# A kernel of two transformer blocks on one core: new orders for the first block's mixers, and a router in column tiles

## The chip, the core and the metric

The kernel is one program for one core of a Trainium2 chip. It is written by hand: each engine (PE for matrix products, DVE for vectors, ACT for activation functions, SP for starting transfers) has a list of instructions of its own and waits for semaphores. The metric is the device time of one execution in microseconds, lower is better. The kernel before took 2264.09 us, the median of three runs (2259.77 to 2264.97).

## The reference

256 tokens of width 1024 in float32 go through two blocks of two layers each. The first block, cut to what matters here:

```
for l in range(2):
    z = rms_norm(x, g_mix[l]) @ w_in[l]              # 2840 columns
    y = concat(chunked_spatial_gating(z_a),          # "ga": 4 heads
               rwkv7_time_mix(z_b),                  # "rw": 4 heads, a recurrence over time
               nsa_attention(z_c))                   # "at": 8 heads, compressed, selected, window
    x = x + y @ w_out[l]
    h = rms_norm(x, g_ffn[l])
    x = x + (swiglu(h) if l == 0 else moe_swiglu(h)) # dense, then 8 experts
    x = x + a gated projection of p[l]               # "ple"
```
```
def moe_swiglu(x, router_w, router_b, w1, w3, w2):
    logits = x @ router_w + router_b
    top_v, top_i = lax.top_k(logits, 2)
    gate = sum of one_hot(top_i) * softmax(top_v)
    return sum over e of gate[:, e] * (silu(x @ w1[e]) * (x @ w3[e])) @ w2[e]
```

The second block (other mixers, a dense network of width 2816 in each layer) is the same in both kernels.

## The kernel before, in words

Tokens lie in two tiles of 128 (`i` = 0, 1). The program is a sequence of stages: mixers of layer 0, dense network, ple, mixers of layer 1 (`pe_mixers1(l)`, `act_mixers1(l)`, `dve_mixers1(l)` for both layers), routing, experts, ple, second block. Nothing plans the order: it is written out by hand in these three functions, one list per engine, and each engine runs its list strictly in order. A step is a small function with the name of its engine in front. Steps of one chain on different engines meet through named signals (`wait_ge`, `then_inc`). So the place of a step in a list says what it runs beside, and a step that waits holds everything behind it on its engine.

The mixers. `win(t, i)` is a product of normalised tokens with 384 of the 2840 input columns (152 for the last `t` = 7); `(0,)` and `(1,)` are its two halves, between which other work can stand. `z(t, i)` is ACT's copy out of PSUM. Beside these products run three chains. *ga*: gelu, a layer norm per head (`ga_norm`, `ga_affine`), one mixing product. *rw*: shift and mix (`rw_shift`, `rw_mix`), low-rank products (`rw_lora`), cumulated decays (`rw_cum`), four turns, products within chunks (`rw_prod`), an inverse by five levels (`rw_lx`, copy, `rw_xlx`, `rw_inverse`, next `rw_level`), then `rw_hv`, `rw_solve`, `rw_inside`, `rw_chunks`, `rw_state` 1 and 2, `rw_read`, `rw_out`, `rw_bonus`, `rw_finish`, which signals `rw.out`. *at*: turns of queries and keys, a compressed attention (`at_compress` to `at_cmp_values`), and six units `u` of the selected and the window attention, each `scores`, `mask`, `max`, `exp`, `gate`, `scale`, `turn_w`, `pt`, `values`. When all is there, `turn_mixed1` and `copy_mixed1` turn the results of ga and rw, `wout1_low(i)` multiplies them with half of `w_out`, and `wout1_high(i)` adds the part of the attention once `at.out` is copied.

The routing (layer 1). `pe_route` makes logits in two tiles of tokens: 16 products with the normalised tokens as stationary operand and 8 router columns as moving one. DVE finds the two best experts of each token (`ro_sel`, signal `route.selected`). PE counts tokens per expert and their places by products with triangular and full matrices of ones (`route.counts`). DVE then sorts the experts by their number of tokens (`route.order`, read by SP, which starts the loads of expert weights), finds places and `mo_pick0`, and writes the largest number (`route.most`). Between its waits PE does the ple products of layer 1, `pe_ple_product(0)` and `(1)`. `pe_mo_gather(0)` collects the tokens of the first expert. Then every worker engine reads `route.most` and branches: the usual path is `gathered`. There, `pe_mo_up(g)` for wave 0 waits for the whole first piece of weights (`moe.up0`, 2 MB). The ring holds five pieces.

## Time and profile before

| | |
|---|---|
| median of 3 runs | 2264.09 us |
| profiled execution | 2261.43 us |
| its span | 2260.1 us |
| PE busy | 2166.3 us, 96% of the span |
| DVE busy | 695.9 us, 31% |
| ACT busy | 427.8 us, 19% |
| chain that ended last | PE 87%, DVE 7%, ACT 3%, DMA 1%, issue 1% |

The span is the time from the first to the last instruction in the records. Layer 0's mixers end at about 227 us, layer 1's lie between 504 and 710, the routing between 715 and 740, the experts between 740 and 1460. A float32 product shows as two records. Source lines say little here, as all instructions pass through one helper (line 89), so rows are told apart by time, engine and operands. The granted clock of PE is given as a share of 2.4 GHz; its two levels are 1.00 and 0.50.

### The profile page before, as it was taken

How to read it: one execution, taken by the hardware profiler on the slowest of the kernel's cores; microseconds unless marked ns; L12 is line 12 of the kernel's file. 1: busy time of each engine (PE TensorE's matmuls, PEld its weight loads, DVE VectorE, ACT ScalarE, POOL GpSimd, SP SyncE). 2: the span in 40 equal slices, each digit the busy share in tenths (PEclk: the TensorE clock that was granted, in tenths of full speed). 3: DMA queues.
4: the chain of work that ended last, by engine and by line, in shares of the span. 5: the costliest groups of instructions: out<-in, count | busy, mean ns of one | idle time of the engine just before them, and what ended most of it. 6: DMA issues, size and time to landing. Idle time of an engine off the chain costs nothing.

```text
span 2260.1 us, 28897 instructions
## 1 busy us (share of the span) xinstructions
PE 2166.3 (96%) x12233; PEld 1260.8 (56%) x12233; DVE 695.9 (31%) x1453; ACT 427.8 (19%) x961; POOL 0.2 (0%) x4
## 2 busy tenths in 40 slices
PE   8988999999979999999999999999999999999998
PEld 5664777765755433333333233365677776657775
DVE  2563365223662100110100001035436633730001
ACT  2464000022462000000000001142310002330001
POOL 0000000000000000000000000000000000000000
PEclk9998999999979999999999999999999999999999
DMA  5221985143301999889999999533199631238300
GB/s 223 86 104 73 423 338 198 34 192 132 107 35 73 423 384 395 345 355 424 403 409 423 377 422 396 209 125 111 56 388 390 225 151 71 88 143 331 142 35 19
DMA packets 55431, 523.38 MB, mean 232 GB/s; under 512 B 6400, under 2 KB 6912, under 8 KB 17152
## 3 DMA queue, kind: packets, MB, share of 16 engines
q1 hardware_dynamic: 46080, 471.13, 51.6%
q10 hardware_dynamic: 9216, 50.34, 5.9%
q8 instruction: 99, 1.62, 0.3%
q14 instruction: 36, 0.29, 0.0%
HBM read 520.39 MB, written 1.05 MB: 231 GB/s over the span
## 4 chain that ended last, share of the span: by engine, by line
PE 87%; DVE 7%; ACT 3%; DMA 1%; issue 1%; SPq 0%; DVEq 0%; ACTq 0%
PE ps L89 87%; DVE ring L89 5%; ACT ring L89 2%; DVE stat L89 1%; DVE transposed L89 1%; DVE natural L89 0%; DMA ring<-in_ple_gate 0%; DMA ring<-in_moe 0%; DVE residual L89 0%; ACT L89 0%; DMA constants<-in_const 0%; DVE gates L89 0%; ACT natural L89 0%; ACT z L89 0%; DVE z L89 0%
## 5 line engine op out<-in xcount | busy, mean ns | idle before, releaser
L89 PE MATMUL ps<-ring 128*32 128x512 f32 (+10 forms) x3812 | 538.8, 515 | 12.7 <-issue 5.5
L89 PE MATMUL ps<-ring,transposed 128*128 128x384 f32 (+4 forms) x1408 | 479.0, 497 | 7.6 <-ACT transposed L89 3.5
L89 PE MATMUL ps<-ring,z 128*32 128x512 f32 (+3 forms) x2048 | 475.8, 584 | 0.3 <-ACT z L89 0.3
L89 PE MATMUL ps<-transposed,ring 128*128 128x256 f32 x2112 | 466.4, 379 | 3.9 <-DVE transposed L89 3.9
L89 PEld LDWEIGHTS ps<-transposed,ring 128*128 128x128 f32 x2112 | 401.1, 190 | 84.4 <-issue 33.1
L89 PEld LDWEIGHTS ps<-ring,transposed 128*128 128x128 f32 x1408 | 264.8, 193 | 197.0 <-issue 67.3
L89 PEld LDWEIGHTS ps<-ring 128*32 128x32 f32 (+4 forms) x3812 | 200.0, 129 | 295.2 <-issue 271.9
L89 DVE TENSOR_TENSOR z<-z,ps 128x256 f32<-128x256 f32 (+2 forms) x138 | 57.5, 417 | 895.6 <-ACT z L89 873.7
L89 PEld LDWEIGHTS ps<-ring,z 128*32 128x32 f32 (+2 forms) x2048 | 174.1, 139 | 247.9 <-issue 241.7
L89 ACT ACTIVATE z<-ps 128x256 f32<-128x256 f32 (+2 forms) x143 | 54.9, 384 | 906.5 <-PE ps L89 906.3
L89 ACT COPY z<-ps 128x256 f32<-128x256 f32 (+6 forms) x154 | 63.4, 412 | 625.4 <-PE ps L89 623.9
L89 DVE SCALAR_TENSOR_TENSOR natural<-z,modulation,natural 128x384 f32<-128x384 f32 x160 | 99.0, 619 | 5.6
L89 ACT ACT_TABLE_LOAD x63 | 80.8, 1283 | 9.7 <-DVE routing L89 5.7
L89 ACT ACTIVATE ring<-ring,stat 128x256 f32<-128x256 f32 (+1 forms) x144 | 65.4, 454 | 29.6 <-DVE stat L89 24.6
L89 DVE TENSOR_TENSOR residual<-residual,ps 128x512 f32<-128x512 f32 x44 | 30.2, 687 | 112.9 <-PE ps L89 112.3
L89 PEld LDWEIGHTS ps<-constants,z 128*128 128x128 f32 (+2 forms) x315 | 32.7, 150 | 54.9 <-issue 51.6
L89 DVE SCALAR_TENSOR_TENSOR ring<-ring 128x256 f32<-128x256 f32 (+2 forms) x126 | 59.4, 471 | 4.5
L89 PE MATMUL ps<-diagonal,residual 128*128 128x128 f32 x320 | 41.7, 287 | 15.7 <-DVE diagonal L89 15.7
L89 PE MATMUL ps<-constants,ring 128*128 128x128 f32 (+3 forms) x292 | 39.9, 312 | 14.2 <-ACT ring L89 13.2
L89 PEld LDWEIGHTS ps<-diagonal,residual 128*128 128x128 f32 x320 | 39.9, 200 | 22.1 <-DVE diagonal L89 19.5
L89 PE MATMUL ps<-constants,z 128*128 128x128 f32 (+2 forms) x315 | 49.0, 284 | 2.1 <-DVE natural L89 2.1
L89 ACT COPY ring<-ps 128x512 f32<-128x512 f32 (+5 forms) x78 | 41.1, 527 | 47.7 <-PE ps L89 44.1
(123 smaller groups left out, 901.6 us busy)
## 6 DMA issues: line engine op xcount, KB each, us to landing
ring<-in_moe SPq DMA_DIRECT2D x88, 2048.0 KB, 13.5
ring<-in_ffn SPq DMA_DIRECT2D x66, 1536.0 KB, 14.0
ring<-in_moe SPq DMA_DIRECT2D x88, 1024.0 KB, 12.6
ring<-in_w_in SPq DMA_DIRECT2D x26, 1536.0 KB, 6.4
z<-in_ada ACTq DMA_DIRECT2D x48, 768.0 KB, 6.2
ring<-in_w_out SPq DMA_DIRECT2D x12, 1536.0 KB, 6.7
natural<-in_ada ACTq DMA_DIRECT2D x16, 768.0 KB, 8.3
ring<-in_ple_gate SPq DMA_DIRECT2D x4, 1536.0 KB, 9.7
```

What stands on the lines that cost most here:

```text
L89: self.ins = None if self.book.counting else op(*args, **kw)
```

## The change

The steps of the three lists of `mixers1` stand in another order. The router's logits are made in four column tiles, kept, and summed over the tiles by a second product; three new operations on DVE (`dve_router`) lay out the router's columns. Counts are made before the places and have a signal of their own, and the ple products are split in four and stand elsewhere. The first piece of expert weights is loaded in two parts of 1 MB; the first wave waits for the first part, and for the second (`moe.up0`) behind its fourth k.

```diff
+    rt = Carve(slot(9))
+    rt_weights, rt_sum, rt_parts = rt(KD, 32), rt(NE), rt(SEQ)
+    def dve_router():
+        dve.wait_ge(*outs1(1))
+        dve(V.memset, rt_weights, 0.0)
+        dve(V.tensor_copy, rt_weights[:, :, 0:NE], column(1, "router").rearrange("p (k e) -> p k e", k=KD))
+        dve(V.tensor_reduce, rt_sum, C("ident").rearrange("p (q e) -> p e q", q=4)[:, 0:NE, :], AXX, ALU.add).then_inc("route.router")
     def pe_route():
-        for i in range(NT):
-            for k in range(KD):
-                mm(ps[:, 4, NE * i:NE * i + NE], xt[:, k, i * P:(i + 1) * P], router[:, k, :], k == 0, k == KD - 1)
+        for k in range(KD):
+            q = k % 4
+            mm(ps[32 * q:32 * q + 32, 4, 0:SEQ], rt_weights[:, k, :], xt[:, k, :], k < 4, k >= 4)
+        pe.then_inc("route.parts")
+        pe.wait_ge("route.parts.kept")
+        for i in range(NT):
+            mm(ps[:, 5, NE * i:NE * i + NE], rt_parts[:, i * P:(i + 1) * P], rt_sum)
         pe.then_inc("route.logits")
-        pe_ple_product(0)
+        pe_ple_product(0, 0)
         pe.wait_ge("route.selected")
-        mm(ps[:, 5, 0:NE], C("tri"), ro_sel[:, 0, :])
-        mm(ps[:, 5, NE:2 * NE], C("tri"), ro_sel[:, 1, :], True, False)
-        mm(ps[:, 5, NE:2 * NE], C("ones"), ro_sel[:, 0, :], False, True)
-        mm(ps[:, 5, 2 * NE:3 * NE], C("ones"), ro_sel[:, 0, :], True, False)
-        mm(ps[:, 5, 2 * NE:3 * NE], C("ones"), ro_sel[:, 1, :], False, True)
+        for i in range(NT):
+            mm(ps[:, 5, 2 * NE:3 * NE], C("ones"), ro_sel[:, i, :], i == 0, i == NT - 1)
         pe.then_inc("route.counts")
-        pe_ple_product(1)
+        mm(ps[:, 4, 0:NE], C("tri"), ro_sel[:, 0, :])
+        mm(ps[:, 4, NE:2 * NE], C("tri"), ro_sel[:, 1, :], True, False)
+        mm(ps[:, 4, NE:2 * NE], C("ones"), ro_sel[:, 0, :], False, True)
+        pe.then_inc("route.places")
+        pe_ple_product(0, 1)
+        pe_ple_product(1, 0)
+        pe_ple_product(1, 1)
         pe_mo_gather(0)
...
     def dve_route():
+        dve.wait_ge("route.parts")
+        dve(V.tensor_copy, rt_parts, ps[:, 4, 0:SEQ]).then_inc("route.parts.kept")
         dve.wait_ge("route.logits")
...
+        dve.wait_ge("route.places")
-        dve(V.tensor_tensor, ro_pv, ps[:, 5, 0:2 * NE].rearrange("p (i e) -> p i e", i=NT), ro_sel, ALU.mult)
+        dve(V.tensor_tensor, ro_pv, ps[:, 4, 0:2 * NE].rearrange("p (i e) -> p i e", i=NT), ro_sel, ALU.mult)
...
-                    sp.wait_ge("ple1.product1")
+                    sp.wait_ge("ple1.product11")
...
+            if (n, part) == (0, "up"):
+                by_half = lambda ap: ap[:, at].rearrange("p (h k n) -> p h k n", h=2, k=2)
+                sp.load(by_half(piece(n))[:, :, 0], by_half(src)[:, :, 0], "first", "moe.first")
+                sp.load(by_half(piece(n))[:, :, 1], by_half(src)[:, :, 1], f"{part}{n % RING_PIECES}", f"moe.{part}{n}")
...
+        if g == 0:
+            pe.wait_ge("moe.first")
...
+                if g == 0:
+                    pe.wait_ge("moe.up0")
```

The PE list of the mixers, from `win(2, 0)` on (the words `pe_`, `rw_`, `at_` are left out; `|` marks a half):

```
before: win20|  shift00 shift10  win20|  win21  win30|  shift01 shift11  win30|  win31  win40  turn_lo
        win41|  lora  win41|  win50  cum  ga_mix  win51|  turn0  win51|  turn1  q0raw q1raw  turn2 turn3
        win60|  prod0 prod1  win60|  win61  first  win70|  lx1  win70|  win71|  xlx1  win71|  turn_k
        lx2  q0rot q1rot  xlx2  pairs0 pairs1  lx3  scores0  xlx3  compress  scores1  cmp_turn_pre
        lx4 xlx4  compressed  lx5 xlx5  turn_w0  hv  cmp_scores  scores2  solve  values0  inside
        turn_w1  cmp_turn  turn_g  scores3  values1  chunks  cmp_values1  turn_w2  cmp_values0  state1
        scores4  values2  state2  read  turn_w3  scores5  values3  turn_mixed1  turn_w4  wout_low0
        values4  turn_w5  wout_low1  values5  wout_high0  wout_high1
after:  win20  win21  win30|  shift00 shift10  win30|  shift01  win31|  shift11  win31|  win40  turn_lo
        win41|  lora  win41|  cum  win50  win51  turn0  win60|  turn1 turn2  ga_mix  turn3  win60|
        prod0 prod1  win61|  q0raw q1raw  first  win61|  win70  win71  lx1  turn_k  xlx1  q0rot q1rot
        lx2  pairs0  xlx2  pairs1  lx3  scores0  xlx3  compress  cmp_turn_pre  scores1
        lx4 xlx4  compressed  lx5 xlx5  turn_w0  hv  solve  scores2  inside  values0  cmp_scores
        turn_w1  turn_g  scores3  chunks  values1  turn_w2  state1 state2  scores4  cmp_turn  read
        cmp_values1  values2  cmp_values0  turn_w3  scores5  values3  turn_mixed1  wout_low0  turn_w4
        wout_low1  values4  turn_w5  wout_high0  values5  wout_high1
```

The parts of the other two lists that differ and that the prediction speaks of:

```diff
 ACT
-  z30 z31  ga_gelu  z40  lo_copy  ga_root  wa  z41  rw_root  z50  decays  turn0  z51  turn1 ...
+  z30 z31  lo  z40  lo_copy  wa  ga_gelu  z41  ga_root  rw_root  decays  z50  turn0 ... turn3  z51
-  exp1  cmp_exp  scale1  pt1  exp2  turn_g  cmp_turn  scale2 ...
+  exp1  scale1  cmp_exp  pt1  exp2  turn_g  scale2  pt2  exp3  cmp_turn ...
-  scale3  pt3  norm_root  exp4  scale4  copy_mixed1  pt4
+  scale3  norm_root  pt3  copy_mixed1  exp4  scale4  pt4
 DVE
-  ga_norm ga_affine  wa keys wx keys2 factors  ga_out  rotate_q pairs  prod0 prod1 first level1
+  wa keys  ga_norm  wx keys2 factors  ga_affine ga_out  prod0 prod1 first level1  rotate_q pairs
-  level4  max0  mask1  hidden  inverse4 level5 kp  gate0 max1  inverse5  hv  cmp_mask  mask2  solve
+  level4  max0  hidden  inverse4 level5 kp  mask1  gate0 max1  inverse5  hv  solve  mask2
-  gate1 max2  cmp_weights  inside  mask3 gate2 max3  chunks  state1  mask4  state2  gate3  max4
+  gate1 max2  inside  cmp_mask cmp_weights  mask3 gate2 max3  chunks  state1 state2  mask4  gate3
-  out bonus finish  mask5 ...
+  out bonus finish  max4  mask5 ...
+  if l == 1: dve_router()     # behind gate5
```

## Rows read from the trace of the kernel before

**Rows 1.** Busy time by stage: us from the start: length, each engine, clock, DMA.
```profile
22.00:205.00 183.00, 163.35 (x1466) 111.76 (x1465) 92.88 (x194) 88.46 (x197) 0.00 (x0) 0.93 0.23 85
509.00:693.00 184.00, 163.45 (x1468) 111.57 (x1467) 92.54 (x192) 85.56 (x189) 0.00 (x0) 0.93 0.23 84
741.00:1460.00 719.00, 719.00 (x4763) 254.19 (x4761) 64.67 (x145) 58.69 (x156) 0.00 (x0) 1.00 0.94 387
```

**Rows 2.** PE timeline, layer 1 mixers: start, length, operation, records, [idle before <- releaser].
```profile
611.34 3.05 PE L89 MATMUL ps<-ring 128*32 128x128 f32 x80
...
627.76 6.42 PE L89 MATMUL ps<-ring 64*64 64x64 f32 x72
...
671.04 1.97 PE L89 MATMUL ps<-constants,natural 128*128 128x128 f32 x8 [4.87 <-DVE natural L89]
...
676.96 9.04 PE L89 MATMUL ps<-ring,transposed 128*128 128x512 f32 x16
```

**Rows 3.** DVE timeline of the same stretch, columns as above.
```profile
616.62 1.42 DVE L89 TENSOR_TENSOR ring<-ps,constants 128x512 f32<-128x512 f32 x2
...
628.96 0.69 DVE L89 COPY z<-ps 128x512 f32<-128x512 f32 x1 [1.96 <-PE ps L89]
632.85 0.41 DVE L89 TENSOR_TENSOR ring<-ps,constants 128x240 f32<-128x240 f32 x1 [3.19 <-PE ps L89]
...
649.35 0.94 DVE L89 COPY ring<-ps 128x128 f32<-128x128 f32 x3
...
659.03 1.26 DVE L89 TENSOR_TENSOR ring<-ring,ps 64x128 f32<-64x128 f32 x4
...
673.02 1.22 DVE L89 TENSOR_REDUCE stat<-ring 128x4 f32<-128x1024 f32 x1
```

**Rows 4.** ACT timeline of the same stretch, columns as above.
```profile
643.19 1.20 ACT L89 COPY ring<-ps 128x512 f32<-128x512 f32 x2 [1.19 <-PE ps L89]
...
673.02 2.13 ACT L89 ACTIVATE ring<-ring,stat 128x256 f32<-128x256 f32 x4 [5.31 <-DVE stat L89]
675.23 1.26 ACT L89 COPY transposed<-ps 128x512 f32<-128x512 f32 x2
...
695.97 0.58 ACT L89 COPY transposed<-ps 128x512 f32<-128x512 f32 x1 [6.69 <-PE ps L89]
```

**Rows 5.** Busy time of two windows, columns as in rows 1.
```profile
634.12:642.06 7.94, 7.12 (x133) 6.00 (x133) 6.33 (x15) 3.62 (x9) 0.00 (x0) 0.84 0.01 2
720.00:727.00 7.00, 7.00 (x18) 3.35 (x17) 2.01 (x9) 0.96 (x3) 0.00 (x0) 0.62 0.00 0
```

**Rows 6.** PE timeline of the routing and the first expert products.
```profile
715.58 4.25 PE L89 MATMUL ps<-layer_cols,transposed 128*128 128x8 f32 x32 [1.22 <-DVE transposed L89]
719.68 6.50 PE L89 MATMUL ps<-ring 128*128 128x512 f32 x8
726.02 1.18 PE L89 MATMUL ps<-routing,constants 128*128 128x8 f32 x10
727.05 3.68 PE L89 MATMUL ps<-ring 128*128 128x512 f32 x8
731.03 3.84 PE L89 MATMUL ps<-z,natural 128*128 128x128 f32 x32 [0.30 <-DVE z L89]
740.37 6.40 PE L89 MATMUL ps<-ring 128*128 128x512 f32 x8 [5.49 <-issue]
```

**Rows 7.** DVE timeline of the routing.
```profile
715.46 1.54 DVE L89 TENSOR_SCALAR natural<-residual,stat 128x1024 f32<-128x1024 f32 x2
719.87 0.17 DVE L89 TENSOR_TENSOR routing<-ps,layer_cols 128x16 f32<-128x16 f32 x1 [2.86 <-PE ps L89]
...
721.70 0.17 DVE L89 TENSOR_SCALAR routing<-routing 128x16 f32<-128x16 f32 x1
...
727.24 0.17 DVE L89 SCALAR_TENSOR_TENSOR z<-ps,constants 128x8 f32<-128x8 f32 x1 [4.95 <-PE ps L89]
```

**Rows 8.** Chain that ended last: the first load of expert weights, issue to landing.
```profile
730.27 7.48 DMA ring<-in_moe
```

More of the change, by code:

```diff
@@ L1602, in pe_route @@
     def pe_route():
         pe.part("route")
-        router = column(1, "router").rearrange("p (k e) -> p k e", k=KD)
-        pe.wait_ge(*(f"ffn1.xt{i}{q}" for i in range(NT) for q in range(2)))
+        pe.wait_ge("route.router", *(f"ffn1.xt{i}{q}" for i in range(NT) for q in range(2)))
+        for k in range(KD):
[3 more added lines that the diff above has]
+        pe.wait_ge("route.parts.kept")
@@ L1632, in dve_route @@
         dve.part("route")
+        dve.wait_ge("route.parts")
+        dve(V.tensor_copy, rt_parts, ps[:, 4, 0:SEQ]).then_inc("route.parts.kept")
         dve.wait_ge("route.logits")
-        dve(V.tensor_tensor, ro_L, ps[:, 4, 0:NT * NE].rearrange("p (i e) -> p i e", i=NT), spread(column(1, "rb"), 1, NT), ALU.add)
+        dve(V.tensor_tensor, ro_L, ps[:, 5, 0:NT * NE].rearrange("p (i e) -> p i e", i=NT), spread(column(1, "rb"), 1, NT), ALU.add)
         dve_beats(ro_sel, ro_L, NE)
@@ L1700, in load @@
             src = d["moe"][p if book.counting else order[x] + p]
-            sp.load(piece(n)[:, at], src[:, at], f"{part}{n % RING_PIECES}", f"moe.{part}{n}")
+            if (n, part) == (0, "up"):
+                by_half = lambda ap: ap[:, at].rearrange("p (h k n) -> p h k n", h=2, k=2)
+                sp.load(by_half(piece(n))[:, :, 0], by_half(src)[:, :, 0], "first", "moe.first")
+                sp.load(by_half(piece(n))[:, :, 1], by_half(src)[:, :, 1], f"{part}{n % RING_PIECES}", f"moe.{part}{n}")
+            else:
+                sp.load(piece(n)[:, at], src[:, at], f"{part}{n % RING_PIECES}", f"moe.{part}{n}")
         for n in range(len(PIECES) + 1):
@@ L1838, in pe_mo_up @@
         pe.part("mo")
-        for _, _, _, block, _ in jobs:
-            pe.wait_ge(f"moe.up{PIECES.index((x, block // 2))}")
+        if g == 0:
+            pe.wait_ge("moe.first")
+        else:
+            for _, _, _, block, _ in jobs:
+                pe.wait_ge(f"moe.up{PIECES.index((x, block // 2))}")
         if w == 0:
@@ L2632, in pe_mixers1 @@
         win(1, 1)
-        win(2, 0, (0,))
+        win(2, 0)
+        win(2, 1)
+        win(3, 0, (0,))
         if l == 0:
@@ L2637, in pe_mixers1 @@
         pe_rw_shift(l, 1, 0)
-        win(2, 0, (1,))
-        win(2, 1)
-        win(3, 0, (0,))
+        win(3, 0, (1,))
         pe_rw_shift(l, 0, 1)
+        win(3, 1, (0,))
         pe_rw_shift(l, 1, 1)
-        win(3, 0, (1,))
-        win(3, 1)
+        win(3, 1, (1,))
         win(4, 0)
@@ L2649, in pe_mixers1 @@
         win(4, 1, (1,))
+        pe_rw_cum(l)
         win(5, 0)
-        pe_rw_cum(l)
-        pe_ga_mix(l)
-        win(5, 1, (0,))
-        pe_rw_turn(l, 0)
-        win(5, 1, (1,))
-        pe_rw_turn(l, 1)
+        win(5, 1)
+        pe_rw_turn(l, 0)
+        win(6, 0, (0,))
+        pe_rw_turn(l, 1)
+        pe_rw_turn(l, 2)
+        pe_ga_mix(l)
+        pe_rw_turn(l, 3)
+        win(6, 0, (1,))
+        pe_rw_prod(l, 0)
+        pe_rw_prod(l, 1)
+        win(6, 1, (0,))
         pe_at_turn_q(l, 0, "raw")
         pe_at_turn_q(l, 1, "raw")
-        pe_rw_turn(l, 2)
-        pe_rw_turn(l, 3)
-        win(6, 0, (0,))
-        pe_rw_prod(l, 0)
-        pe_rw_prod(l, 1)
-        win(6, 0, (1,))
-        win(6, 1)
         pe_rw_first(l)
-        win(7, 0, (0,))
+        win(6, 1, (1,))
+        win(7, 0)
+        win(7, 1)
         pe_rw_lx(l, 1)
-        win(7, 0, (1,))
-        win(7, 1, (0,))
+        pe_at_turn_k(l)
         pe_rw_xlx(l, 1)
-        win(7, 1, (1,))
-        pe_at_turn_k(l)
-        pe_rw_lx(l, 2)
         pe_at_turn_q(l, 0, "rot")
         pe_at_turn_q(l, 1, "rot")
+        pe_rw_lx(l, 2)
+        pe_at_turn_pairs(l, 0)
         pe_rw_xlx(l, 2)
-        pe_at_turn_pairs(l, 0)
         pe_at_turn_pairs(l, 1)
@@ L2801, in act_mixers1 @@
         act_at_exp(l, 3)
+        act_at_cmp_turn(l)
         act_at_out(l, 0)
         act_at_scale(l, 3)
+        act_rw_norm_root(l)
         act_at_pt(l, 3)
-        act_rw_norm_root(l)
+        act_copy_mixed1(l)
         act_at_exp(l, 4)
         act_at_scale(l, 4)
-        act_copy_mixed1(l)
         act_at_pt(l, 4)
@@ L2850, in dve_mixers1 @@
         dve_rw_level(l, 1)
+        dve_at_rotate_q(l)
+        dve_at_pairs(l)
         dve_at_rotate_k(l)
@@ L2860, in dve_mixers1 @@
         dve_at_max(l, 0)
-        dve_at_mask(l, 1)
         dve_at_hidden(l)
@@ L2865, in dve_mixers1 @@
         dve_rw_kp(l)
+        dve_at_mask(l, 1)
         dve_at_gate(l, 0)
@@ L2892, in dve_mixers1 @@
         dve_at_gate(l, 5)
+        if l == 1:
+            dve_router()
         for i in range(NT):
```

89 lines of the change are left out of this document (43 added, 46 removed).

## The prediction

> **What bounds the kernel now.** I read the stages first, with the table of busy times [rows 1]. The span is 2260.1 us, the profiled execution's own time 2261.4, the median of the runs 2264.1, so I make the sum against 2261.4 and add 2.7 at the end. In the expert stage (741 to 1460) PE is busy all 719.0 us while the DMA engines are at 0.94: PE paces it, and when it begins is what counts. The first block's mixers run twice, once per layer, with 163.35 us of PE work in 183.00 and 163.45 in 184.00. So each leaves PE about 20 us idle, and the two passes are alike: I work out layer 1 and count it twice. The diff touches these two stretches and the routing between them and the experts; nothing behind it has other work.
>
> Inside a mixer stage I went to the PE timeline [rows 2]. PE runs without large gaps as long as there are win products; its idle time lies behind them. The largest gap is 4.87 us before the 8 transposes at 671.04, which wait for DVE's product of `dve_rw_finish` (`rw.out`); a second one follows, while ACT scales (2.13 us at 673.02 [rows 4]) what turn_w(4) needs. The late half is therefore set by the rw chain on DVE and ACT, and the question is how much earlier `rw.out` comes and whether PE then has what it needs.
>
> **The mixers, part by part (layer 1).**
>
> *Win products and early rw steps.* No instruction is added. The lists change only what PE does while DVE and ACT work. Counting PE's work in the new order, `pe_rw_prod` comes within half a microsecond of where it was; the first levels too. I take 0, bounds -1.5 to +1.5. The cover is win 5 to 7, which now stand closer together. If DVE's factors were late there, up to the block of ga_norm that now stands inside the rw steps would show (five operations like the 0.69 us at 628.96 [rows 3] and two small ones, 3.9 us).
>
> *Levels 4 and 5.* `dve_at_mask(1)`, 1.42 us at 616.62 [rows 3], stood before `dve_rw_inverse(4)`; it moves behind level 5. DVE's part of the chain is shorter by that: -1.4 us at the hv copy (628.96 becomes 627.5). Bounds 0 to -2.7, as ACT's exp(0) may hold cx of level 5 instead.
>
> *hv to solve.* From the end of the hv copy, 629.65, to the solve products, 634.1 (start of the first window in [rows 5]), PE did cmp_scores and scores(2) (the 6.42 us at 627.76 are hv and both of these [rows 2]). The solve now follows hv directly: -4.5. So u is ready 5.9 us earlier.
>
> *Given back at once.* cmp_scores now stand behind solve, scores(2), inside and values(0), and ACT's `act_at_cmp_exp` now stands between scale(1) and pt(1); pt(1) and all ACT work behind it, exp(2) and the copy of gT among it, wait for cmp_scores. PE's work from the hv copy: 7.1 us for solve, values(0), inside (PE busy in the window, 0.84 of full clock [rows 5]), less about 1.3 for the half clock, plus 6.42 less 1.0 for hv: 11.2 us, so cmp_scores end at 628.2 + 11.2 = 639.4. DVE's mask and shift, three operations like the 0.41 us at 632.85 [rows 3], and exp add 1.7: pt(1) starts at 641.1, against 643.19 [rows 4]. -2.1 is what remains of the 5.9. `pe_rw_chunks` waits for gT, so DVE's chunk copies (649.35 [rows 3]) come at 647.2.
>
> *States and read.* From 649.35 to 659.03, where `dve_rw_out` begins, DVE does chunks, state 1, mask(4), state 2, gate(3), max(4). max(4) is 1.22 + 0.17 = 1.4 (the same reduction as at 673.02 [rows 3]) and goes behind `rw_finish`. mask(4) is still ahead of rw_out, but no longer between state 1 and 2, so PE's state products and its read are hidden less badly; I take 0.4 for it. -1.8: rw.out at 671.0 - 2.1 - 1.8 = 667.1.
>
> *Turn, copy, wout.* Before, PE turned at 671.04, but ACT was still to do scale(4) before `act_copy_mixed1` at 675.23 [rows 4], and `pe_wout1_low(0)` began at 676.96, 6.0 us after rw.out. Now the copy stands ahead of exp(4): turns of tile 0 (half of 1.97), copy (half of 1.26), then the second half of the turns: 2.1 us. -3.9. wout low(0) begins at 669.2, 7.8 us earlier.
>
> *Given back at the end.* Turn_w(4) was done before 676.96 and now follows low(0): +1.0 (8 transposes, 1.97 at half clock [rows 2]). values(5) now is behind high(0), so high(1) waits for the copy `at.out` of 0.58 [rows 4] and the hand-overs around it: +0.9. ACT's chain for units 4 and 5 now starts after the copy: twice scale 2.13 and pt 1.20 [rows 4], exp at some 2.6 (the same four rows, each with its sum), DVE's gates and PE's turns between them, about 16 us. Its cover is low(0), low(1), high(0), 48 records at 3.68/8 us [rows 6], 22 us. It is hidden, with 6 us to spare. Net 7.8 - 1.9 = 5.9; I take 6 per layer, 12 in all, bounds 2 and 9 each.
>
> **The routing.** [rows 6] PE: logits 4.25 (16 products, 32 records), product(0) 6.50, counts 1.18, product(1) 3.68, gather 3.84, then 5.49 idle until the experts begin. In this gap lies the branch on `route.most`; the weights of the first piece landed before its end, at 730.27 + 7.48 = 737.75 [rows 8]. So PE's arrival at the branch, 734.87, plus 5.5 sets the start, and not the load. Earlier orders for the loads alone win nothing.
>
> New: 8 products in four column tiles. The nearest row is 611.34, 80 records with 128 columns in 3.05 us [rows 2]; 16 records of 256 columns take by it 1.2 us. They end at 716.8, DVE is on `dve_natural` to 717.0 [rows 7], the new copy of 128x256 takes 0.42 (like the 0.41 us of 240 columns [rows 3]), two small products 0.5, and the addition of the bias starts at 718.3, not 719.87. From it to `route.selected` 2.0 us as before [rows 7]: 720.3. PE is done with product(0, 0) (half of 3.68) at 719.9 at full, 721.1 at half clock. Counts thus at 720.3 to 721.1; DVE goes on at about 721.3 instead of 727.24. The order of the experts comes 6 us earlier, the picks too. But now PE is the bound: places and counts 1.2, three half products 5.5, gather 3.84, from 720.7: 731.2, and at 0.62 of the clock for as long as in 720 to 727 [rows 5] some 2 us more. It reaches the branch at 731 to 733.5, not 734.87: -2.7 in the middle, bounds -4 and +0.5. `dve_router`'s three operations run on DVE while PE does the last wout products and cost nothing; without that cover about 0.8 us. The split load costs SP one more issue of 0.5 us, behind the first landing; piece 3 now waits for the last product, but 8 MB are queued ahead of it.
>
> The row for column tiles shows them side by side. The Trainium skill, TensorEngine Tiling (Array Packing), Key Properties, says that a change of tiling mode drains the engine, and under PSUM Bottleneck that after a fourfold gain the copy out of PSUM can become the bound. That speaks against this part: two mode changes and one more copy before the logits. By the row the first stage takes 1.2 us and the chain to the bias gains 1.6; if the tiles did not overlap at all, 8 products of 256 columns at half of 3.68/4 us each are 3.7 us, the bias addition comes at 720.8, and the routing gains 0.2 instead of 2.7.
>
> **Sum.** -12 - 2.7 = -14.7: 2246.7 for a profiled execution, 2249.4 against the median. I forecast 2249.
>
> **The rivals.**
> A (my forecast, own range 2243 to 2255): 0.60.
> B, more than that: without the long idle stretches the clock stays up. At 676.96 sixteen records took 9.04 us, where 2 x 3.68 [rows 6] is the price at full clock: 1.7; the turns of 1.97 would take half, 1.0; the early part gives up to 1. Per layer 3.5 more, and the routing at its bound 4: 12 + 7 + 4 = 23: 2241. For it: PE idle falls from 20 us. Against: most of the 4.87 us wait for rw.out [rows 2] only moves earlier. 0.17.
> C, the mixers give nearly nothing since the rw chain is bound by ACT, where no work leaves: 1.5 each, routing 1.5: 2259.5. For it: ACT's wait for cmp_exp is new. Against: the copy of mixed1 alone gains 3.9. 0.15.
> D, tiles of the router do not overlap and the rest holds: 2252, inside A's range; 0.03, by the skill's drain rule as worked out above.
> E, slower. Place: PE's stretch from hv to the end of cmp_scores, 11.2 us of products on which now all that ACT has left hangs. PE waits before it for scale(0); if the clock then falls to half and stays there, the stretch takes 11.2 us more, pt(1) starts at 652.3, and the layer is 11.2 - 6 = 5.2 us slower than before: 2264.1 + 10.4 - 2.7 = 2271.8. It decides from 6 us of loss, when more than half of the stretch is at half clock in both layers. Against: the mean clock in 634.12 to 642.06 was 0.84 [rows 5]. 0.05.
>
> **Numbers.** A difference under about 0.3% (6.8 us, below 2257.3 or above 2270.9) can't be told from none: three runs spread 5.2 us. A, B, D and a fifth of C are faster, the rest of C and a fifth of E the same, the rest of E slower: faster 0.83, same 0.13, slower 0.04. The range reaches to B's and C's typical times: 2240 to 2259.
>
> **What would show it.** rw.out near 4 us earlier within its stage; low(0) within 2.5 us of it; PE idle per mixer stage about 14 us instead of 20; a gap of 0.9 us before the last 8 wout products; ACT idle before the cmp_exp of 240 columns; counts within 6 us of the first router product; PE at the experts 5.5 us after the gather, and 3 us sooner relative to the last xt; the expert stage again 719 us. It is wrong if scale(4) or pt(5) keep PE waiting between the wout products, if a DMA wait appears at the first expert wave, or if PE's half-clock time grows.

## The result, and the profile after

The changed kernel takes 2249.5 us (median of 14 runs, 2243.27 to 2257.21), the kernel before, on the same chip, 2262.62 (14 runs). The ratio is 0.9949, 95% interval 0.9938 to 0.9960: 11.5 us faster, between 9.0 and 14.0. By the medians the gain is 13.1 us; the ratio weighs all the runs, and the gains below go by it. The prediction was 2249. Its total is right; several of its terms are not, and they cancel. The profiled execution took 2252.66 us, its span is 2251.2, so it is one of the slower ones.

Busy time by stage of the changed kernel, columns as in [rows 1]:

```profile
22.00:202.00 180.00, 165.05 (x1466) 112.10 (x1465) 92.89 (x194) 84.73 (x193) 0.00 (x0) 0.93 0.25 89
506.00:688.00 182.00, 166.96 (x1476) 113.72 (x1475) 92.51 (x192) 82.98 (x187) 0.00 (x0) 0.93 0.24 85
733.00:1452.00 719.00, 718.80 (x4763) 254.23 (x4761) 64.64 (x145) 58.86 (x157) 0.00 (x0) 1.00 0.94 385
```

The expert stage is the same 719 us, and PE still paces it. Each mixer stage leaves PE about 15 us idle instead of 20. Layer 1 of this trace stands 3.25 us earlier than before at its start (layer 0's gain), so 3.25 is added wherever its times are compared with rows of before. PE from the last level on:

```profile
618.37 3.68 PE L89 MATMUL ps<-gates 64*64 64x64 f32 x64 [1.73 <-ACT gates L89]
622.36 1.97 PE L89 MATMUL ps<-constants,ring 128*128 128x128 f32 x8 [0.31 <-ACT ring L89]
...
626.23 1.96 PE L89 MATMUL ps<-z,gates 64*64 64x128 f32 x32 [0.80 <-DVE z L89]
...
633.14 3.97 PE L89 MATMUL ps<-ring 64*128 64x15 f32 x32
...
660.68 1.09 PE L89 MATMUL ps<-constants,ring 128*128 128x128 f32 x8 [2.90 <-ACT ring L89]
663.54 2.08 PE L89 MATMUL ps<-ring 64*128 64x256 f32 x8 [1.77 <-ACT ring L89]
665.55 1.97 PE L89 MATMUL ps<-ring,z 128*64 128x256 f32 x8
667.46 1.69 PE L89 MATMUL ps<-constants,natural 128*128 128x128 f32 x8
669.34 7.10 PE L89 MATMUL ps<-ring,transposed 128*128 128x512 f32 x16 [0.20 <-ACT transposed L89]
...
694.93 7.13 PE L89 MATMUL ps<-ring,transposed 128*128 128x512 f32 x16 [0.69 <-ACT transposed L89]
```

Solve (626.23) now follows hv, and the compressed scores (633.14) come after it. But turn_w(3), scores(5) and values(3) (660.68 to 667.5) stand in front of the mixed tile's turns (667.46), with 2.90 and 1.77 us of waits for ACT. DVE and ACT of the same stretch: the hv copy, the chunk copies, rw_out and the last product of the rw chain; then, on ACT, cx of level 5 behind exp(0), pt(1), the copy of tile 0's attention output (`act_at_out(0)`) with scale(3) behind it, and the copy of mixed1:

```profile
625.48 0.69 DVE L89 COPY z<-ps 128x512 f32<-128x512 f32 x1 [2.70 <-PE ps L89]
...
645.82 0.94 DVE L89 COPY ring<-ps 128x128 f32<-128x128 f32 x3
...
654.24 1.26 DVE L89 TENSOR_TENSOR ring<-ring,ps 64x128 f32<-64x128 f32 x4
...
665.37 0.69 DVE L89 TENSOR_TENSOR natural<-ring 128x512 f32<-128x512 f32 x1
```
```profile
617.95 0.83 ACT L89 COPY gates<-ps 128x256 f32<-128x256 f32 x2
...
638.96 1.20 ACT L89 COPY ring<-ps 128x512 f32<-128x512 f32 x2
...
657.82 0.58 ACT L89 COPY transposed<-ps 128x512 f32<-128x512 f32 x1 [4.05 <-PE ps L89]
658.49 2.13 ACT L89 ACTIVATE ring<-ring,stat 128x256 f32<-128x256 f32 x4
...
668.61 1.26 ACT L89 COPY transposed<-ps 128x512 f32<-128x512 f32 x2 [5.12 <-PE ps L89]
```

The routing on PE:

```profile
707.78 1.07 PE L89 MATMUL ps<-transposed,ring 128*32 128x256 f32 x16 [1.22 <-DVE transposed L89]
709.79 4.63 PE L89 MATMUL ps<-ring 128*128 128x8 f32 x8 [0.94 <-DVE ring L89]
714.22 2.14 PE L89 MATMUL ps<-routing,constants 128*128 128x8 f32 x10
716.21 7.23 PE L89 MATMUL ps<-ring 128*128 128x512 f32 x12
723.28 3.73 PE L89 MATMUL ps<-z,natural 128*128 128x128 f32 x32
732.30 1.19 PE L89 MATMUL ps<-ring 128*128 128x512 f32 x1 [5.29 <-issue]
```

From the first router product to the experts it takes 24.5 us, before 24.8 [rows 6]. The clock stood at 1.2 GHz for 10.2 us from 709.7 on. By this one trace the routing gave nothing, and that was my first theory. The experiments show that it was this execution.

### The profile page after: what moved, and what is told of

Same layout as the page of the kernel before. It is cut to its first block, busy times and chain, and to the rows that moved or that the text cites. A ratio compares the mean times of both kernels' runs of the same rounds, so it can differ in the third digit from the quotient of the medians.

```text
span 2251.2 us, 28880 instructions
## 1 busy us (share of the span) xinstructions
PE 2165.6 (96%) x12221; PEld 1260.3 (56%) x12221; DVE 696.9 (31%) x1457; ACT 422.7 (19%) x957; POOL 0.2 (0%) x4
## 4 chain that ended last, share of the span: by engine, by line
PE 89%; DVE 7%; ACT 3%; issue 1%; DMA 1%; SPq 0%; DVEq 0%; ACTq 0%
PE ps L89 89%; DVE ring L89 4%; ACT ring L89 1%; DVE transposed L89 1%; DVE natural L89 1%; DVE stat L89 0%; DMA ring<-in_ple_gate 0%; DVE residual L89 0%; ACT transposed L89 0%; ACT L89 0%; ACT natural L89 0%; DVE gates L89 0%; DMA constants<-in_const 0%; ACT stat L89 0%; ACT z L89 0%
## 5 line engine op out<-in xcount | busy, mean ns | idle before, releaser
L89 PE MATMUL ps<-ring 128*32 128x512 f32 (+11 forms) x3816 | 544.6, 519 | 16.0 <-ACT ring L89 5.8
L89 PE MATMUL ps<-transposed,ring 128*128 128x256 f32 (+1 forms) x2128 | 467.4, 379 | 5.2 <-DVE transposed L89 5.2
L89 PEld LDWEIGHTS ps<-transposed,ring 128*128 128x128 f32 (+1 forms) x2128 | 401.6, 189 | 85.8 <-issue 34.5
## 6 DMA issues: line engine op xcount, KB each, us to landing
ring<-in_moe SPq DMA_DIRECT2D x87, 2048.0 KB, 13.3
```

What stands on the lines that cost most here:

```text
L89: self.ins = None if self.book.counting else op(*args, **kw)
```

## The experiments

All were timed against the kernel before, in the same rounds and on the same chip. Gain is one minus the ratio, times 2262.3 us; by the intervals it is known to within 2 to 4 us.

| kernel | median us (runs, lowest to highest) | ratio, 95% interval | gain us |
|---|---|---|---|
| changed kernel | 2249.50 (14, 2243.27 to 2257.21) | 0.9949 (0.9938 to 0.9960) | 11.5 |
| mixers_only | 2252.88 (5, 2250.44 to 2255.37) | 0.9965 (0.9952 to 0.9978) | 7.9 |
| routing_only | 2256.46 (9, 2253.69 to 2258.38) | 0.9976 (0.9967 to 0.9986) | 5.4 |
| early_new | 2259.03 (12, 2254.45 to 2263.56) | 0.9983 (0.9973 to 0.9992) | 3.8 |
| late_new | 2252.08 (6, 2245.54 to 2254.61) | 0.9954 (0.9940 to 0.9969) | 10.4 |
| tail_old | 2254.37 (12, 2254.01 to 2261.67) | 0.9975 (0.9966 to 0.9984) | 5.7 |
| cmp_scores_first | 2253.38 (12, 2250.06 to 2264.11) | 0.9972 (0.9959 to 0.9985) | 6.3 |
| out_late | 2250.23 (5, 2244.6 to 2256.54) | 0.9942 (0.9929 to 0.9955) | 13.1 |
| route_fill | 2248.36 (6, 2243.75 to 2253.05) | 0.9941 (0.9928 to 0.9953) | 13.3 |
| no_tiles | 2254.17 (6, 2250.73 to 2257.41) | 0.9959 (0.9947 to 0.9972) | 9.3 |
| one_load | 2247.21 (6, 2243.98 to 2255.44) | 0.9937 (0.9921 to 0.9953) | 14.3 |
| chunks_first | 2249.60 (6, 2246.64 to 2251.93) | 0.9945 (0.9933 to 0.9957) | 12.4 |
| shorter_chain | 2246.04 (6, 2244.69 to 2252.45) | 0.9936 (0.9922 to 0.9951) | 14.5 |

The runs of one kernel spread over 4 to 14 us, and not evenly: of tail_old's twelve nine lie within 0.5 us and three 5 to 8 us above. So ratio and median can tell different gains, for tail_old 5.7 and 8.0, for cmp_scores_first 6.3 and 9.0. Where the spread comes from stays open.

Stages of their traces, in us: in layer 1 the start of solve, of rw_out, of the last rw product (its result is rw.out) and of wout low(0), counted from the start of PE's turn of tile 1 ahead of the layer's mixers; the length of both mixer stages, layer 0 from its first turn, layer 1 from the turn of tile 1, to the next stage's first turn, and PE's idle time in them; from the first router product to the end of the gather and to the experts; and the part up to the gather's end in which the granted clock was at 1.2 GHz:

| kernel | solve | rw_out | last rw | low(0) | mixers 0 + 1 | PE idle | gather end | experts | 1.2 GHz |
|---|---|---|---|---|---|---|---|---|---|
| before | 130.1 | 155.0 | 166.3 | 172.9 | 419.7 | 40.2 | 19.3 | 24.8 | 6.8 |
| changed | 125.5 | 153.5 | 164.6 | 168.6 | 411.8 | 31.4 | 19.2 | 24.5 | 10.2 |
| mixers_only | 125.8 | 155.7 | 166.7 | 170.7 | 410.9 | 31.8 | 19.3 | 24.5 | 6.8 |
| routing_only | 129.9 | 155.0 | 166.3 | 172.9 | 422.3 | 40.7 | 14.8 | 20.5 | 0.0 |
| early_new | 131.8 | 156.3 | 167.5 | 174.2 | 422.0 | 38.7 | 16.0 | 21.5 | 3.4 |
| late_new | 125.7 | 154.2 | 165.1 | 168.7 | 413.9 | 31.7 | 14.8 | 21.4 | 0.0 |
| tail_old | 125.4 | 154.9 | 166.2 | 172.9 | 419.1 | 36.5 | 14.8 | 21.0 | 0.0 |
| cmp_scores_first | 129.9 | 156.2 | 167.1 | 170.3 | 414.4 | 34.9 | 16.0 | 21.3 | 3.4 |
| out_late | 125.4 | 156.3 | 167.2 | 169.8 | 418.2 | 33.8 | 14.8 | 21.2 | 0.0 |
| route_fill | 125.4 | 156.3 | 167.2 | 171.2 | 416.3 | 34.9 | 13.8 | 20.4 | 0.0 |
| no_tiles | 125.1 | 157.4 | 168.3 | 171.9 | 418.0 | 34.6 | 18.7 | 24.3 | 6.8 |
| one_load | 125.9 | 155.9 | 166.8 | 170.7 | 413.8 | 33.6 | 14.8 | 19.7 | 0.0 |
| chunks_first | 125.3 | 154.5 | 165.4 | 168.7 | 412.4 | 32.6 | 14.8 | 20.2 | 0.0 |
| shorter_chain | 125.4 | 152.2 | 162.0 | 166.9 | 411.0 | 31.7 | 14.8 | 19.7 | 0.0 |

The five kernels with the same mixer lists (changed, mixers_only, route_fill, no_tiles, one_load) differ by 5.9 us in layer 0 and 3.3 in layer 1, so single cells say little, and columns are read by groups of kernels.

**mixers_only and routing_only: the two halves of the change.** The lists of `pe_mixers1`, `act_mixers1` and `dve_mixers1` alone, or all the rest alone.

> The kernel before with the changed kernel's three lists of the mixers, and nothing of the routing. My theory after reading the changed kernel's trace: the mixers bring almost all of it, and the routing next to nothing (in the trace its stretch from the first router product to the experts went from 24.8 to 24.5 us). The whole change is 13.1 us by medians; then this kernel is 12 us faster than before, 2250.6 us, and rw.out's transposes and wout low(0) stand as early in their stages as in the changed kernel. Rival, the prediction's own split: the routing is worth 2.7, so this one stands at 2262.6 - 10.4 = 2252.2. A second rival, that the two gains are not additive because the earlier experts only wait for their weights: 2249.5, the same as the whole change.

> The kernel before with the changed routing, the three added router operations and the split load, and the mixers' lists as they were. My theory: PE's work in the routing, 19.2 us in both traces, sets when the branch is reached; earlier counts only take DVE off that path. Then it gains 0.3 to 1 us: 2262.0. Rival, the prediction's step: PE loses its waits, -2.7: 2259.9. Third: the four column tiles and their copy cost more than they save once the clock is at half, +1: 2263.6. In its profile the last gather product ends 19 us after the first router product by my theory, 16.5 by the rival.

7.9 us (5.0 to 10.9) and 5.4 us (3.2 to 7.5): my theory of an idle routing falls. PE in routing_only:

```profile
718.25 1.07 PE L89 MATMUL ps<-transposed,ring 128*32 128x256 f32 x16 [1.22 <-DVE transposed L89]
720.26 2.43 PE L89 MATMUL ps<-ring 128*128 128x8 f32 x8 [0.94 <-DVE ring L89]
722.98 1.28 PE L89 MATMUL ps<-routing,constants 128*128 128x8 f32 x10 [0.29 <-DVE routing L89]
724.11 5.40 PE L89 MATMUL ps<-ring 128*128 128x512 f32 x12
729.35 3.73 PE L89 MATMUL ps<-z,natural 128*128 128x128 f32 x32
738.75 5.19 PE L89 MATMUL ps<-ring 128*128 128x512 f32 x8 [5.66 <-issue]
```

The same instructions as in the changed kernel, at full clock: counts 4.7 us after the first router product, gather done after 14.8. The last columns of the table show this as the usual case: 14.8 to 16.0 in nine traces with exactly these PE products, and 19.2 in the changed kernel's alone, which ran at 1.2 GHz for 10.2 us of it.

**early_new and late_new: which part of the mixers' order.** The cut lies behind level 5.

```diff
 early_new = changed kernel, but from here on the lists of before; late_new the reverse
     PE:  pe_at_turn_w(l, 0, ...)    ACT: act_at_compressed(l)    DVE: dve_at_gate(l, 0)
```

> The changed kernel, but the later part of the three lists (on PE from turn_w(0) and hv on, on ACT from the compressed keys on, on DVE from gate(0) on) in the order of before. What stays new in the mixers is the order up to level 5, mask(1) behind it among it. My theory: the early order is worth nothing or little, since the hv copy came only 0.2 us earlier against the layer's own start; the time is that of before plus what the routing gives, 2261.5, at most 2 us below it. Rival: the early order sets half of the gain (PE's win products closer together keep its clock up): 2256.

> The changed kernel, but the first part of the three lists (up to level 5, mask(1) ahead of inverse(4) again) in the order of before; the part from hv on is the new one. My theory: all of the mixers' gain sits here, solve behind hv, states and read, and the copy of mixed1 ahead of exp(4): 2250.5, within 1.5 us of the changed kernel. Rival: half sits in the early part, 2256. If both halves alone give little and only together give the gain (each then waits for what the other has late), this one and its counterpart sum to much less than 11 us.

early_new gains 3.8 with the new routing, which alone gains 5.4: no gain of the early order can be told. late_new, at 10.4 of 11.5, holds nearly all. As expected.

**tail_old: the last step undone.**

```diff
 DVE  dve_at_gate(l, 3)
+     dve_at_max(l, 4)
      dve_rw_out(l) ...
-     dve_at_max(l, 4)          # was behind dve_rw_finish
 ACT -     act_copy_mixed1(l)
      act_at_exp(l, 4)
      act_at_scale(l, 4)
+     act_copy_mixed1(l)
 PE  -     pe_wout1_low(l, 0)
      pe_at_turn_w(l, 4, ...)
+     pe_wout1_low(l, 0)
```

> The changed kernel with its last step of the mixers undone: max(4) ahead of rw_out, the copy of mixed1 behind scale(4), turn_w(4) ahead of wout low(0). The prediction took 1.4 for max(4) and 3.9 for the copy, less 1.0 for turn_w(4); in the changed kernel's trace low(0) comes 3.3 us after the turns begin, against 6.0 before. My theory: per layer 2.7 + 1.4 - 1.9 = 2.2 us are lost, 4.4 in all: 2254. Rival: PE has all its products of the end to do anyway and scale(4) hardly delays the copy now, so that nothing is lost: 2249.5. In the trace rw.out's transposes would come 1.4 us later by my theory, and low(0) another 2.7.

5.7 us of gain are left, and the routing alone gives 5.4; 2254.37 was forecast at 2254. By the ratios this step is 5.8 of the 6.1 us by which the mixers' lists better routing_only, and the intervals leave room for some 3 us elsewhere; by the medians tail_old is 2.1 us under routing_only. PE of tail_old:

```profile
669.28 1.44 PE L89 MATMUL ps<-constants,natural 128*128 128x128 f32 x8 [0.26 <-DVE natural L89]
673.44 1.97 PE L89 MATMUL ps<-constants,ring 128*128 128x128 f32 x8 [2.73 <-ACT ring L89]
675.20 14.72 PE L89 MATMUL ps<-ring,transposed 128*128 128x512 f32 x32
```

PE waits 2.73 us for scale(4) with the mixed tile already turned. In the table the four kernels with the old tail have low(0) 6.7 us after the last rw product, those with the new tail and otherwise this order 3.6 to 4.0; the mixers take 419.7, 422.3, 422.0 and 419.1 us against 410.9 to 418.0 in six with the new one (changed, mixers_only, late_new, route_fill, no_tiles, one_load): means 420.8 and 414.1, 6.7 us apart. A rival is the clock: the four were at 1.2 GHz for 51 to 61 us of their mixers (mean 57), the six for 44 to 51 (47). But PE's idle time alone differs by 6.1 us (means 39.0 and 33.0), and its busy time, 381.7 and 381.1 us, by 0.6 us, so the clock can hold little of the 6.7. tail_old's own idle time, 36.5, lies between the two groups: some of the gain in idle time isn't of this step.

**cmp_scores_first: what hangs on solve.** `pe_at_cmp_scores(l)` right behind `pe_rw_hv(l)`.

> The changed kernel with the compressed scores on PE right behind hv and ahead of solve, as before; ACT and DVE unchanged. It tells what hangs on solve and what on pt(1). Theory of the prediction (given back at once): pt(1), held by the compressed scores, sets gT and the chunks, and the 5.9 us by which u is earlier are mostly lost there; then putting these scores first costs solve 3 us and nothing behind it, and pt(1) comes up to 2 us earlier: 2249.5 +- 1.5, or up to 2 us better. Rival: the rw chain through solve paces, and 3 us per layer are lost: 2255.

Solve falls back to 129.9, and rw_out starts at 156.2, inside the 153.5 to 157.4 of the seven traces with solve at 125.1 to 125.9 and the new order behind it (changed, mixers_only, late_new, out_late, route_fill, no_tiles, one_load). So no gain of an early solve at rw_out can be told. PE of cmp_scores_first:

```profile
623.31 6.60 PE L89 MATMUL ps<-ring 64*64 64x64 f32 x64
629.85 3.65 PE L89 MATMUL ps<-z,gates 64*64 64x128 f32 x32
```

hv with the compressed scores and solve ran at 1.2 GHz here (solve 3.65 us instead of 1.96). The time, though, shows 6.3 us of gain against 11.5, with intervals that touch (0.9959 to 0.9985, 0.9938 to 0.9960). Its traced stages don't show that loss, but the traced execution, 2251.56, is the third fastest of twelve that reach to 2264.11; where the loss would lie stays open.

**out_late: the output behind pt(3).** `act_at_out(l, 0)` directly ahead of `act_copy_mixed1(l)`.

> The changed kernel with the first attention output's scaling on ACT (it waits for the compressed values, and ACT stands idle 4.05 us in front of it in layer 1, with scale(3) queued behind it) moved behind pt(3). PE is idle 2.90 us before turn_w(3) and 1.77 us before scores(5) there. My theory: scale(3) goes 4 us earlier and PE loses these waits; but rw.out comes from DVE and stays, so only what PE has left to do behind it gets shorter: 2 us per layer, 2245.5. Rival: the end is set by rw.out and the wout products alone: 2249.5. Second rival: the norm's root and its table load now come before the output and hold it, high(1) waits: +1 per layer.

No difference from the changed kernel that can be told. The turns follow the last rw product at 0.7 us instead of 2.1 in layer 1, so the wait moved; what the trace gained at low(0) it lost to the clock, low(0) taking 9.05 us for 7.10:

```profile
665.90 1.97 PE L89 MATMUL ps<-ring,z 128*64 128x256 f32 x8
670.33 1.97 PE L89 MATMUL ps<-constants,natural 128*128 128x128 f32 x8 [2.46 <-DVE natural L89]
672.21 9.05 PE L89 MATMUL ps<-ring,transposed 128*128 128x512 f32 x16
```

**route_fill: PE's waits in the routing filled.**

```diff
+        pe_ple_product(0, 1)                     # behind ffn1.xt01
         parts (8 products in column tiles)
+        pe_ple_product(0, 0)
         logits
-        pe_ple_product(0, 0)
+        pe_ple_product(1, 0)
         counts, places
-        pe_ple_product(0, 1); pe_ple_product(1, 0)
         pe_ple_product(1, 1); pe_mo_gather(0)
```

> The changed kernel with PE's waits in the routing filled by the half products that stand behind it: product(0,1) before the router's products, where PE waits 1.22 us for xt, product(0,0) between them and the logits, where it waits 0.94 us for the copy, product(1,0) behind the logits. My theory: PE's work from the last turn to the branch is then one stretch, and the branch is reached 1.5 to 2 us sooner, more if the clock stays up: 2247.5. Rival: the picks come from the order's chain on DVE, which moves back by the 1.9 us that stand ahead of the logits, and nothing is won: 2249.5. Third: experts start earlier and wait for their weights.

```profile
711.07 1.07 PE L89 MATMUL ps<-transposed,ring 128*32 128x256 f32 x16
712.07 4.15 PE L89 MATMUL ps<-ring 128*128 128x512 f32 x12
...
721.02 3.84 PE L89 MATMUL ps<-z,natural 128*128 128x128 f32 x32 [1.42 <-DVE z L89]
731.42 6.06 PE L89 MATMUL ps<-ring 128*128 128x512 f32 x8 [6.56 <-issue]
```

The first rival fits: the filled waits come back as 1.42 us before the gather, for DVE's picks, and a wait of 6.56 follows it, the longest of all. No gain can be told (2248.36, intervals alike).

**no_tiles: early counts without column tiles.**

```diff
-  8 products of 256 columns into four column tiles; copy; two products with rt_sum
+  for i in range(NT):
+      for k in range(KD): mm(ps[:, 5, NE*i:NE*i + NE], xt[:, k, tile i], rt_weights[:, k, 0:NE], ...)
```

> The changed kernel with the router's products as before (16 products of 8 columns each over 128 rows, straight to the logits, no copy), and with the early counts, the products in halves and the split load left in. In the routing at full clock the stretch from the first router product to the last gather product is 14.8 us in two traces of the new routing and 19.3 in three of the old one or at half clock. My theory: by rows the tiles save 1.2 us to the bias addition (3.07 against 4.29), which is not PE's bound alone, and the early counts the rest of the 4.5: this kernel is 1 to 1.5 us slower than the changed one, 2250.8. Rival: the column tiles are the gain, the counts nothing: 2254. Second rival: the copy and the second product cost what the tiles save: 2249.5.

The time doesn't decide: the median is the rival's, but 9.3 us of gain are 2.2 fewer than the changed kernel's, and the interval holds 1.5 us of loss as well as 4. The trace speaks for the rival:

```profile
712.32 5.66 PE L89 MATMUL ps<-ring,transposed 128*128 128x8 f32 x32 [1.22 <-DVE transposed L89]
717.83 3.32 PE L89 MATMUL ps<-ring 128*128 128x512 f32 x4
720.99 1.18 PE L89 MATMUL ps<-routing,constants 128*128 128x8 f32 x10
722.03 5.40 PE L89 MATMUL ps<-ring 128*128 128x512 f32 x12
```

All three kernels with the 16 products of 8 columns (this, before, mixers_only) are at 1.2 GHz for 6.8 us before the gather's end and reach it after 18.7 to 19.3 us, whatever the order of the counts. Of the eleven with column tiles eight show no time at 1.2 GHz there, and two show 3.4 us; these ten reach the gather's end after 13.8 to 16.0. The eleventh is the changed kernel's. Its trace gives the clock a price, as the same instructions took 19.2 us with 10.2 at 1.2 GHz, 16.0 with 3.4, and 14.8 with none: 0.35 to 0.43 us for each. By an estimate from these, the 6.8 us of the kernel before cost 2.4 to 2.9 of the 4.5 us between 19.3 and 14.8, and the order and the shorter products give the rest.

**one_load: the first weights in one load.** `moe.up0` whole, as before.

> The changed kernel with the first expert's weights in one load, as before, and its first wave waiting for the whole of it. My theory, as in the prediction: the load is not on the path; in the traces its first half lands 8.0 us and its second half 5.4 us before the experts begin (and even before the change the whole landed 2.6 us ahead of them), so nothing changes: 2249.5 within 1 us. Rival: the shorter first load is what lets the early counts pay, and without it 1 to 3 us are lost: 2251.5.

Nothing is lost. The wait between the gather and the experts is 4.9 us here and in shorter_chain, which has one load too, against 5.3 to 6.6 in the ten traces with the split load; but before and mixers_only, with one load and the late counts, had 5.5 and 5.2. The split costs up to a microsecond there, if anything (what ends this wait is told in the last section). In the time it can't be told (2247.21).

**chunks_first: the chunk products ahead of unit 3's scores.**

```diff
 PE   pe_at_cmp_scores, +pe_rw_turn_g, pe_at_turn_w(1), +pe_rw_chunks, pe_at_scores(3), pe_at_values(1),
      pe_rw_state(1), pe_at_turn_w(2), pe_rw_state(2)
 ACT  +act_rw_turn_g, act_at_cmp_exp, act_at_pt(1), act_at_exp(2)
 DVE  dve_at_gate(2), +dve_rw_chunks, dve_at_mask(3), dve_rw_state(1), dve_at_max(3), dve_rw_state(2)
```

> The changed kernel with a shorter way from u to rw.out: on PE the turn of g right behind the compressed scores and the chunk products ahead of scores(3), on ACT the copy of gT ahead of cmp_exp, on DVE gate(2) and the chunk copies ahead of mask(3) and max(3). In the traces solve comes 4.5 us earlier by the new order, and rw_out (the first product with the state) only 0 to 1.5 us: DVE's chunk copies wait for the chunk products, which stand behind scores(3), which waits for pt(1). My theory: this is what gave the gain back, and here it is found again: rw_out 2.5 to 4.5 us earlier within layer 1, low(0) as much, and 2 to 3 us per layer in the time: 2244.5. Rival: the attention chain on ACT, whose mask(3) and max(3) now come up to 3 us later, sets the end, turn_w(3) and scores(5) come too late, and the time stays or is up to 3 us worse: 2251.

DVE of chunks_first: the chunk copies, the last state, mask(4), rw_out.

```profile
642.58 0.94 DVE L89 COPY ring<-ps 128x128 f32<-128x128 f32 x3
...
650.42 0.55 DVE L89 TENSOR_SCALAR ring<-ring 128x64 f32<-128x64 f32 x2
652.42 1.42 DVE L89 TENSOR_TENSOR ring<-ps,constants 128x512 f32<-128x512 f32 x2 [1.45 <-PE ps L89]
...
654.42 1.26 DVE L89 TENSOR_TENSOR ring<-ring,ps 64x128 f32<-64x128 f32 x4
```

Counted from the turn of tile 1 the chunk copies come at 142.6 us, in the changed kernel at 145.0, and rw_out comes no earlier: mask(4) stands ahead of it and waits 1.45 us for scores(4), and these for pt(2). Attention sets the place, as the rival had it, but at a step that I had not named. 12.4 us of gain, as the changed kernel.

**shorter_chain: the whole rw chain freed.** chunks_first with one load, and:

```diff
 DVE  +dve_rw_bonus (3 operations, scratch rw_t2)  dve_rw_hv ...
      dve_rw_inside  +dve_rw_bonus_v (2 operations)  dve_at_cmp_mask ...
      dve_rw_state(2)  +dve_rw_out  dve_at_mask(4)  dve_at_gate(3)  -dve_rw_bonus  dve_rw_finish
 PE   pe_rw_state(2), +pe_rw_read, pe_at_scores(4), pe_at_cmp_turn, ...,
      pe_at_turn_w(3), +pe_turn_mixed1, pe_at_scores(5), pe_at_values(3), pe_wout1_low(0)
 ACT  act_at_cmp_turn, +act_rw_norm_root, act_at_out(0), act_at_scale(3), act_at_pt(3)
```

> The kernel with one load for the first weights, with the order of chunks_first, and three more edits of the rw chain: the bonus (3.0 us of DVE that stood between rw_out and the last steps) is computed with its own buffer as scratch and moved into DVE's waits, its first three operations ahead of the hv copy (2.70 us idle there), its last two ahead of the compressed mask (2.50 us idle); rw_out and PE's read go ahead of mask(4), gate(3) and scores(4), which waited for pt(2); the norm's root goes ahead of the output and scale(3) on ACT, and PE turns the mixed tile ahead of scores(5). My theory: the one thing that moves the end of a mixer is when PE gets the turned mixed tile, and it is set by DVE's chain from the chunks on: in the trace of chunks_first the last product of that chain starts at 665.33, 24 us after the scores of unit 3 on PE; here it starts 3 to 4.5 us earlier in its layer, low(0) 3 us, and both layers together give 6: 2241.5, that is 1.0% under the kernel before, 0.4% under the changed one. Rival: attention (scale(3), turn_w(3), scores(5) on ACT and PE) is the bound at the same place and low(0) or the products behind it wait for it: 2247, the time of one_load. Second rival: the clock takes it, since PE then has less to do in the same stretch: more half clock, 2249.

The lowest time of all, 2246.04; 14.5 us under the kernel before (11.1 to 17.6), but not told apart from the changed kernel or from one_load. In the trace the last rw product comes 4.8 us earlier than in one_load in layer 1, and low(0) 3.8; in layer 0 low(0) did not come earlier, since the turns there wait behind turn_w(3) until 3.2 us after rw.out is written. What holds it now is the rival's place, ACT's scale(3) and PE's turn_w(3) in front of the turns, and scores(5) behind them; in layer 1:

```profile
663.31 1.97 PE L89 MATMUL ps<-constants,ring 128*128 128x128 f32 x8 [2.90 <-ACT ring L89]
665.07 1.53 PE L89 MATMUL ps<-constants,natural 128*128 128x128 f32 x8
666.57 1.13 PE L89 MATMUL ps<-ring 64*128 64x256 f32 x8
```

## Why the prediction was right, and which of its steps were not

- *Early part, 0:* right as far as the runs can tell. early_new gains no more than the routing alone.
- *Levels 4 and 5, -1.4:* -0.2 (hv copy at 625.48 + 3.25 = 628.7, against 628.96 [rows 3]). The bound that the prediction named held: ACT copies cx of level 5 only at 617.95, behind exp(0), and PE waits 1.73 us for it. Then the products of level 5 and turn_w(0) ran at 1.2 GHz.
- *hv to solve, -4.5:* right, 4.2 to 5.0 in the table. *Given back, 3.8 of 5.9:* the step that failed most. In the changed kernel's trace pt(1) came 1.0 earlier instead of 2.1 and the chunk copies 0.3 instead of 2.1, and over the traces nothing is left: counted from the turn of tile 1, eight kernels with the early solve start the chunk copies at 145.0 to 147.8 us, three with the late one (before, routing_only, early_new) at 145.3 to 146.6. Seven of the eight, with the new tail too, start rw_out at 153.5 to 157.4 (mean 155.6), the three at 155.0 to 156.3. The chunk products stand behind scores(3), which wait for pt(1); chunks_first, which puts them in front, has its chunk copies at 142.6.
- *States and read, -1.8:* mis-sized. From the chunk copies to rw_out the old order takes 9.7 us in each trace and layer, the new one 8.4 to 9.6, on the mean 8.9. The 1.4 for max(4) is there (tail_old, which puts it back, takes 9.9 and 10.0). The 0.4 for mask(4) had the wrong sign: between the two states it had filled a wait of DVE, which waits 0.55 to 0.9 us before each state now, where it waited 0.83 once, and in most traces 0.2 to 0.8 for scores(4) before mask(4) besides. With the step before, rw.out was forecast 3.9 us earlier and did not come earlier: the last rw product starts at 166.6 us on the mean of the seven, at 166.7 on that of the three.
- *Turn, copy, wout, -3.9:* right in kind, -2.7 to -3.1 in layer 1: the turns stand behind scores(5) and values(3), which wait for pt(3), and in the changed kernel start 1.4 us after rw.out is written. tail_old, which undoes this and the move of max(4), shows that most of the mixers' gain goes with them, or all of it.
- *Given back at the end, +1.9:* both parts are there (turn_w(4) 1.09 us, high(1) waits 0.69 us), but low(0) to the next turns takes 32.6 us as before (32.7), since low(0) itself ran at 2.4 GHz, 7.10 us, where it took 9.04 [rows 2]. That is the piece of rival B that came true.
- *Sum for the mixers, -12:* mis-sized, 7.9 by the runs' times and 6.7 by the traces' stages. All of it comes behind rw.out, some 3 us per layer for the 2 forecast there; the 3.9 per layer ahead of it did not come. C's amount for the whole was refuted, but its reason, that the chain behind solve waits for attention's ACT work, fits what is missing.
- *Routing, -2.7:* mis-sized, 5.4 (3.2 to 7.5). The bias addition starts 2.7 us after the first product in the nine other traces with the changed kernel's PE products (3.07 in its own), as forecast, for 4.29 before. The counts start after 4.7 us where the clock stayed up, the early end of the forecast. What I had added on top, 2 us for half clock, is what goes: with column tiles the clock mostly stays at 2.4 GHz. The gather ends 4.5 us sooner, not 2.7. D is refuted: 16 records took 1.07 us. The tiles did overlap, and the copy of 0.42 us with its waits (0.94 us of PE) is paid back. The Trainium skill, TensorEngine Tiling (Array Packing), PSUM Bottleneck, says that after a fourfold gain the copy may become the bound; by these rows it stands on the path without setting it, and what the drain between two tiling modes (Key Properties there) costs no run here shows apart from those waits.
- *Experts 5.5 us after the gather:* 4.9 to 6.6. *Rival E:* refuted; from the end of the hv copy to the end of the compressed scores it took 10.9 us (626.17 to 637.11) for the 11.2 forecast, and no layer became slower.
- *The signs:* PE's idle time of 15 us, the gap before the last wout products (0.69), ACT's wait before the compressed exp (3.77 us), counts within 6 us (not in the changed kernel's trace, 6.4, but in the others) and the expert stage of 719 us came. rw.out 4 us earlier did not, and low(0) came 3.3 us behind it instead of within 2.5. These two told of the failed steps.

So 12 + 2.7 was forecast, and 7.9 + 5.4 by the two halves. The total was right because the rw chain gave less and the clock in the routing more, and that is luck. So is 1.5 us of how near it came: the three runs that the forecast started from have a median of 2264.1, all 14 one of 2262.6.

## What to carry to other kernels

A chain that is shortened at its head gains nothing if something of another chain stands in each engine's list further down: follow it to the last wait before the common end, and price that wait first. Here a step of three moved lines gave most of the gain of the mixers, or all of it, and of the rest of their new order no gain can be told. And read a stage from several executions before giving it a price; one trace said that the routing gains 0.3 us, the runs said 5.
